# Two 256-column weight chunks multiplied as one 512-column operand, token tile by token tile, at the start of stages and in differential attention

## The reference

```python
def swiglu(x, wg, wu, wd):                       # 4 times, hidden width 2816
    return (jax.nn.silu(x @ wg) * (x @ wu)) @ wd

def sq_relu_mlp(h, w1, w2):                      # 4 times, hidden width 4096
    return jnp.square(jax.nn.relu(h @ w1)) @ w2

def diff_mixer(h, w_in, lam_p, norm_g, w_out, lambda_init, cos, sin):
    proj = h @ w_in                              # 1024 x 3072: q, k, v
    q = partial_rope(proj[..., :hq].reshape(b, t, DIFF_HEADS, 2, DIFF_D), cos, sin)
    k = partial_rope(proj[..., hq:2 * hq].reshape(b, t, DIFF_HEADS, 2, DIFF_D), cos, sin)
    v = proj[..., 2 * hq:].reshape(b, t, DIFF_HEADS, 2 * DIFF_D)
    lam = jnp.exp(jnp.sum(lp[0] * lp[1])) - jnp.exp(jnp.sum(lp[2] * lp[3])) + lambda_init
    o = diff_attention(q, k, v, lam)
    ...
    return o.reshape(b, t, hq) @ w_out

def second_block(x, ...):
    for i in range(4):                           # mixers: gdn, mlstm, diff, gdn
        x = x + rms_norm(mixer(rms_norm(x)), ...)
        x = x + rms_norm(sq_relu_mlp(rms_norm(x), mlp_w1[i], mlp_w2[i]), ...)
```

## Time and profile before

| what | value |
|---|---|
| median of 3 runs | 2362.12 us (2359.69 to 2362.32) |
| the profiled execution | 2360.35 us, its span 2358.6 us |
| PE busy | 2325.4 us, 99%, x16820 |
| DVE busy | 1567.7 us, 66% |
| ACT busy | 1157.1 us, 49% |
| POOL busy | 159.1 us, 7% |
| granted clock of PE | 0.999 |
| DMA | 405.14 MB, mean 172 GB/s |

### The profile page before, as it was taken

One profiled execution on the slowest core, in us unless ns is written; L12 is line 12 of the kernel. 1 busy time (PEld: TensorE's weight loads), 2 busy tenths in 40 slices (PEclk: granted clock), 3 DMA queues, 4 the chain that ended last, 5 costly groups with the idle time before them and its releaser, 6 DMA issues. The chain is left out here.

```text
span 2358.6 us, 39266 instructions
## 1 busy us (share of the span) xinstructions
PE 2325.4 (99%) x16820; PEld 2062.5 (87%) x16820; DVE 1567.7 (66%) x2133; ACT 1157.1 (49%) x1573; POOL 159.1 (7%) x177
## 2 busy tenths in 40 slices
PE   9999999999999999999999999999999999999998
PEld 8889888888889888899888899888898888998887
DVE  5566775666576865768666657766677656867665
ACT  5444744435435644466554445534465334665432
POOL 0100000020000100002210000100001001012000
PEclk9999999999999999999999999999999999999999
DMA  7766355666655466453265644556445565433662
GB/s 247 244 214 137 108 186 189 214 187 214 209 148 150 127 210 208 145 168 109 73 214 189 205 154 143 181 194 213 154 142 177 187 206 156 139 110 108 205 210 94
DMA packets 320829, 405.14 MB, mean 172 GB/s; under 512 B 48720, under 2 KB 281264, under 8 KB 320656
## 3 DMA queue, kind: packets, MB, share of 16 engines
q1 hardware_dynamic: 314992, 383.50, 51.6%
q0 software_dynamic: 5664, 19.13, 2.6%
HBM read 401.55 MB, written 1.05 MB: 171 GB/s over the span
## 5 line engine op out<-in xcount | busy, mean ns | idle before, releaser
L468 DVE TENSOR_TENSOR w_lo<-raw,w_hi 128x2048 fp32r<-128x2048 f32 (+1 forms) x355 | 796.4, 2267 | 60.5 <-ACT w_hi L461 59.6
L461 ACT CAST w_hi<-raw 128x2048 fp32r<-128x2048 f32 (+1 forms) x355 | 672.1, 1894 | 303.4 <-PE ps L484 227.6
L512 PE MATMUL ps<-aT,w_hi 128*128 128x512 f32 x2048 | 511.3, 392 | 0.0
L512 PEld LDWEIGHTS ps<-aT,w_hi 128*128 128x128 f32 x2048 | 373.3, 188 | 70.2
L482 PE MATMUL ps<-w_hi,h_hi 128*128 128x512 f32 x864 | 339.2, 393 | 0.7 <-DVE h_lo L1970 0.6
L483 PE MATMUL ps<-w_lo,h_hi 128*128 128x512 f32 x864 | 337.4, 391 | 0.0
L484 PE MATMUL ps<-w_hi,h_lo 128*128 128x512 f32 x864 | 336.3, 389 | 0.0
L482 PE MATMUL ps<-w_hi,aT 128*128 128x256 f32 (+2 forms) x992 | 300.6, 303 | 6.8 <-DVE aT L910 4.6
L514 PEld LDWEIGHTS ps<-aT,w_lo 128*128 128x128 f32 x2048 | 279.4, 190 | 20.0
L484 PE MATMUL ps<-w_hi,aT 128*128 128x256 f32 (+2 forms) x992 | 294.0, 296 | 0.0
L483 PE MATMUL ps<-w_lo,aT 128*128 128x256 f32 (+2 forms) x992 | 294.0, 296 | 0.0
(11 more groups left out here) (397 smaller groups left out, 2687.0 us busy)
## 6 DMA issues: line engine op xcount, KB each, us to landing
raw<-in_mlp_w SPq DMA_DIRECT2D x124, 1024.0 KB, 5.3
raw<-in_ffn_wg SPq DMA_DIRECT2D x43, 1024.0 KB, 5.3
raw<-in_ffn_wu SPq DMA_DIRECT2D x43, 1024.0 KB, 5.3
raw<-in_ffn_wd SPq DMA_DIRECT2D x40, 1024.0 KB, 4.9
raw<-in_gdn_w_in SPq DMA_DIRECT2D x32, 1024.0 KB, 5.9
raw<-in_mlstm_w_in SPq DMA_DIRECT2D x12, 1024.0 KB, 5.4
raw<-in_diff_w_in SPq DMA_DIRECT2D x12, 1024.0 KB, 5.2
raw<-in_w_in SPq DMA_DIRECT2D x8, 1024.0 KB, 5.2
```

Source lines behind the costliest of these rows:

```text
L461: nc.scalar.copy(used_part(hi_slot(n), n), used_part(raw_slot(n), n)).then_inc(hi_ready, 1)
L468: nc.vector.tensor_tensor(used_part(lo_slot(n), n), used_part(raw_slot(n), n), used_part(hi_slot(n), n).bitcast(F32), ALU.subtract).then_i ...
L512: nc.tensor.matmul(ps[:, bank + ft, :], hi[:, k, c], aT[:, k, :], start=k == 0, stop=False)
```

## The change

A new function `open_paired` takes the place of `open_stage` in both mixers of the first block, in the three feed-forward stages of the first block behind the first, in all four MLPs and in differential attention. Bank t now holds tile t of both chunks (one in each half), where bank c held both tiles of chunk c. Tile 0 begins as before, four k of each chunk apart; from then on `pair_steps` multiplies both chunks at once: high parts of two neighbouring slots are read as one operand of 2 x 256 columns. Where the two low parts stand in other order than the high ones (a ring of 5 slots beside one of 4), the low matmul stays two of 256. `weights_used` counts both chunks at the end of the pair. In stages that begin inside the norm of the first block, three pair steps stand ahead of the turns of tile 1, else two.

Differential attention also pairs its chunks 2, 3 and 8, 9, with ACT copying by tile. In the MLP the second hidden tile is now turned inside the first rows chunk (bank 7), and the fifth chunk's product waits for its low part in the middle; DVE and ACT take up its split behind those of chunk n0+6. The mixers 1 to 3 of the second block have their first turns inside the last bank of the MLP ahead (`turn_mixer`), one half of tile 0 (both in differential attention), and `open_stage` takes two steps more ahead of tile 1's turns in the mlstm mixer and the last gdn mixer.

```diff
+    def pair_steps(pe, n, t, steps):
+        swapped = slots_swapped(n)
+        both = ps[:, t, :].rearrange("p (a c) -> p a c", a=2)
+        for k in steps:
+            hi = of_both(w_hi, turn_of[n] % SPLIT, SPLIT, k)
+            x_hi, x_lo = (x_part[:, k, t * P:(t + 1) * P] for x_part in (aT_hi, aT_lo))
+            nc.tensor.matmul(both, x_hi, hi, start=k == 0, stop=False)
+            if swapped[0] == swapped[1]:
+                nc.tensor.matmul(both, x_hi, of_both(w_lo, lo_at[n], RAW, k), start=False, stop=False)
+            else:
+                for a in range(2):
+                    nc.tensor.matmul(ps[:, t, pair_half(n, a)], x_hi, by_cols(lo_slot(n + a))[:, k, :], start=False, stop=False)
+            last = nc.tensor.matmul(both, x_lo, hi, start=False, stop=k == KT - 1)
+        return last
...
+    def open_paired(pe, n, edge, first_tile=None):
...
+        turned_set(0)
+        pe.wait_ge(lo_ready, splits_made[n])
+        one_part(pe, n, 0, 0, first)
+        if edge["early"]:
+            turned_set(1)
+            one_part(pe, n, 0, 0, second)
+        pe.wait_ge(lo_ready, n + 2)
+        one_part(pe, n, 1, 0, first)
+        if edge["early"]:
+            turn_tile(pe, edge, 1)
+            one_part(pe, n, 1, 0, second)
+        else:
+            turned_set(1)
+            ahead = 7 if edge.get("late") else 6
+            pair_steps(pe, n, 0, range(4, ahead))
+            turn_tile(pe, edge, 1)
+            last = pair_steps(pe, n, 0, range(ahead, KT))
...
+        turned_set(2)
+        pair_steps(pe, n, 1, first)
+        turned_set(3)
+        pair_steps(pe, n, 1, second).then_inc(weights_used, 2)
...
     def mlp_tensor(pe, i, edge):
-        def turn_two():
-            turn_hidden(pe, hid0, 0, 2)
-            turn_hidden(pe, hid0 + 1, 1, 6)
-        open_stage(pe, n0, edge)
+        inside = {2: lambda: turn_hidden(pe, hid0, 0, 2), 3: lambda: pe.wait_ge(hid_lo, hid0 + 2)}
+        open_paired(pe, n0, edge)
...
-                hidden_rows(pe, n0 + u, hid0 + s, s)
+                hidden_rows(pe, n0 + u, hid0 + s, s, (lambda: turn_hidden(pe, hid0 + 1, 1, 7)) if s == 0 else None)
...
-            if s == 3:
-                pe.wait_ge(hid_lo, hid0 + 2)
...
     def mlp_vector(dve, i):
...
             for c in split_ahead(MLP_ORDER, u):
                 split_low(dve, n0 + c)
+            if (kind, s) == ("rows", 0):
+                turned_hidden_vector(dve, hid0 + 1, 1, 7)
+                hidden_split(dve, hid0 + 2, 2)
...
+    DF_PAIRED = (0, 2, 8)
...
+            if u in DF_PAIRED:
+                pe.wait_ge(lo_ready, splits_made[n0 + u + 1])
+                pair_steps(pe, n0 + u, 0, range(KT)).then_inc(df_tile.sem, 1)
+            elif u - 1 in DF_PAIRED:
+                pair_steps(pe, n0 + u - 1, 1, range(KT)).then_inc(weights_used, 2)
+            else:
+                tokens_product(pe, n0 + u, u % 2)
...
+    def mixer_turns(q):
+        return ((1, 0), (2, 0)) if factor_behind(q) else ((2, 1),)
```

More of the change, by code:

```diff
@@ new lines, in one_part @@
+    def one_part(pe, n, a, t, steps):
+        hi, lo = by_cols(hi_slot(n + a)), by_cols(lo_slot(n + a))
+        s = slice(t * P, (t + 1) * P)
+        for k in steps:
+            product(pe, ps[:, t, pair_half(n, a)], aT_hi[:, k, s], aT_lo[:, k, s], hi[:, k, :], lo[:, k, :],
+                    a == 0 and k == 0, a == 1 and k == KT - 1)
+    def open_paired(pe, n, edge, first_tile=None):
+        xpass = edge["xpass"]
+        turned_set = lambda e: pe.wait_ge(aT_lo_set.sem, aT_lo_set.count(xpass, e))
+        first, second = range(0, 4), range(4, KT)
+        if not edge["early"]:
+            turn_tile(pe, edge, 0, edge.get("begun", 0))
+        turned_set(0)
[15 more added lines that the diff above has]
+            last = pair_steps(pe, n, 0, range(ahead, KT))
+            if first_tile is not None:
+                last.then_inc(first_tile, 1)
+        turned_set(2)
+        pair_steps(pe, n, 1, first)
+        turned_set(3)
+        pair_steps(pe, n, 1, second).then_inc(weights_used, 2)
@@ L611, in open_stage @@
         tokens_part(pe, n, 0, 0, 1)
+        ahead = 2 if edge.get("late") else 0
+        tokens_steps(pe, n + 1, 1, 0, range(4, 4 + ahead))
         turn_tile(pe, edge, 1)
-        tokens_part(pe, n + 1, 1, 0, 1)
+        tokens_steps(pe, n + 1, 1, 0, range(4 + ahead, KT))
         open_second(pe, n, turned_set)
@@ L636, in last_rows @@
                 for r in range(2):
+                    if b == 3 and mixer_next is not None and (q, r) in mixer_turns(mixer_next):
+                        turn_mixer(pe, mixer_next, mixer_turns(mixer_next).index((q, r)))
                     if b == 3 and turn_next is not None and (q, r) in turns:
@@ L898, in turn_bank, with turned_scalar @@
         last.then_inc(turned.sem, 1)
-    def turned_scalar(act, xpass, t):
-        for half in range(2):
+    def turned_scalar(act, xpass, t, halves=(0, 1)):
+        for half in halves:
             act.wait_ge(turned.sem, turned.count(xpass, 2 * t + half))
@@ L1774, in addnorm_scalar @@
         early = a % 6 == 0
+        inside = range(len(mixer_turns(a + 1))) if into_mixer else ()
         for b in range(4):
@@ L1784, in addnorm_scalar @@
                 x_squares(act, a + 1, 0)
+                turned_scalar(act, xpass, 0, inside)
         if into_mixer:
-            turned_scalar(act, xpass, 0)
+            turned_scalar(act, xpass, 0, [half for half in range(2) if half not in inside])
             x_squares(act, a + 1, 1)
@@ L3339, in prenorm_edge @@
                         half_ready=lambda pe, t, half: pe.wait_ge(mlp_w.sem, mlp_w.count(q // 2, 2 * t + half)))
-        return dict(xpass=xpass, src=H, scaled=not factor_behind(q), early=False, fill={} if q else {(0, None): 3, (1, None): 8}, ready=lambda pe, t: pe.wait_ge(pre_done.sem, pre_done.count(q // 2, t)))
+        return dict(xpass=xpass, src=H, scaled=not factor_behind(q), early=False, begun=len(mixer_turns(q)) if q else 0,
+                    late=q and not factor_behind(q), fill={} if q else {(0, None): 3, (1, None): 8}, ready=lambda pe, t: pe.wait_ge(pre_done.sem, pre_done.count(q // 2, t)))
     def order_of_stages():
```

116 lines of the change are left out of this document (75 added, 41 removed).

## The result

The changed kernel takes 2374.94 us (median of 4 runs, 2373.13 to 2375.66), the one before 2361.11 in the same comparison: a ratio of 1.0058, 95% interval 1.004 to 1.0075. So it is slower by 13.8 us, where 2.4 faster was forecast, and outside the range. The profiled execution has a span of 2372.9 us, 14.3 longer than before.

What follows compares the result with a forecast made beforehand. PE was taken to bound the kernel, busy 2325.4 of 2358.6 us. Gains of 7.8 us less 4.4 in the MLPs and 1.0 in the third feed-forward stage made 2.4 saved: 2359.7 us, range 2353.5 to 2364.5.

Steps and rivals of the forecast that it cites:

- Merged matmuls: In all pair steps, 384 merges of two 256-column matmuls into one of 512, 0.013 us each: 5.1 us saved.
- Openings inside the first block's norm: Both mixers and three feed-forward stages: PE's waits for x go, 3.4 us saved, of which merges are 2.1.
- The wait for the low part: In the profiled norm opening, PE newly waits 0.5 us for the first low part, behind tile 1's turns.
- Turns inside, differential attention: Differential attention's first turns go into the MLP's last bank, chunks pair: 1.9 us saved, 2.2 with the MLP opening behind.
- the wait for ACT's copy at the third chunk: In differential attention, PE waits about 1 us there, where it waited 0.16 before.
- Third feed-forward stage: In the first block, n0+5 lands later: PE waits 0.7 us, and 0.3 at the next chunk, 1.0 in all.
- First turns inside at the mlstm mixer: PE's 0.51 us wait for the first low part is covered: 0.6 us saved; 0.9 with the MLP opening behind.
- The late release in an MLP: Slots freed 2.9 us later, n0+5 lands at T + 6.3 (T: opening's end): 4.4 us lost in four MLPs.
- The chain: In an MLP, from n0+5's landing through ACT's split and copy and DVE's splits to the hidden low part: 9.3 us.
- upper bound of 10.4: The most that later slot release was counted to cost in the four MLPs together, 10.4 us.
- the second rival: In the MLPs, n0+6's landing takes over n0+5's whole delay: 12.3 us lost against 7.8, 2366.6 us; chance 0.11.
- 7.8 of gains without losses: Norm openings 3.4, MLP openings 1.3, first turns at two mixers 1.2, differential attention 1.9: 7.8 us saved.

Runs made afterwards that it cites:

- second experiment: The changed kernel with POOL's two gain loads at each MLP issued only when the MLP's twelfth chunk is used: 2358.17 us, ratio 0.9984.
- first experiment: The changed kernel with the second hidden tile's ACT copy and DVE low part moved ahead of the weight splits in the MLPs: 2358.43 us, ratio 0.9986.
- fourth: The kernel before, with only the slots of an opening's first chunk released later, together with the second's: 2368.48 us, ratio 1.0029.
- tenth experiment: The kernel before with 40 small matmuls at its start and nothing else changed: 2359.93 us, ratio 0.9991.

## Why the prediction was wrong

The forecast is off by 16.2 us: 6.4 of waits in the MLPs, 6.7 behind them, 3.0 in the fourth block's gdn mixer, the rest small.

- **Merged matmuls: right in kind, a third too much.** 384 merges, wide ones 0.227 us apart. Undoing them cost about two thirds of 0.013 us each in the stretches where nothing else moved. (384 times 0.013 is 5.0 and not 5.1; nothing hangs on it.)
- **Openings inside the first block's norm: right.** The waits for x went, the opening of the earlier trace rows takes 12.5 us as worked out, and the five openings gain 3.1 us, 3.4 in the forecast. The wait for the low part in it is 0.3 and not 0.5.
- **Turns inside, differential attention: right as a sum.** -2.3 us against -2.2; the wait for ACT's copy at the third chunk came, with 0.5 and not 1. The price of the turns alone stayed open.
- **Third feed-forward stage: wrong in size.** 1.0 us was counted for waits. The one wait for w_lo is 0.2, and the stage behind its opening is 0.5 longer.
- **First turns inside at the mlstm mixer: right.** The stretch gains 0.7 where 0.9 was forecast, merges included.
- **The late release in an MLP: the step that failed.** The chain was right in place, members and length. Its start was not: "At 406 GB/s half a MB is 1.3 us: n0+5 lands at T + 6.3". The second experiment measures 3.0 us for it. The rate was read in a microsecond in which only weights move; the first gain load has the engines nearly to itself and moves half as much, and the second, in three of the MLPs, was not counted. So each MLP waits 2.2 to 3.5 us in place of 0.8 to 1.2, 10.8 in place of 4.4, just above the upper bound of 10.4. That this sum lies near that bound is luck: the second rival named this size of wait by another way in, n0+6's late landing. DVE's two splits run without a gap, so it was n0+5 that decided. The harm came of the order: with the low part ahead of the splits (first experiment), or with the same late landing and the old order (fourth), no such wait arises.
- **The clock: a step that was missing.** The forecast priced a wait at its length. With three of the four waits the granted clock fell to 0.50 for 3 us and more, 6.7 us in all behind the waits, and with the wait filled it did not. No term and no rival had it, though PE's granted clock of 0.999 was the first thing read.
- **The instruction count: another missing step.** Fewer matmuls moved the places of PE's instruction loads, and with them a wait in the fourth block's mixer: 3.0 us more than forecast. The trace of the kernel before had a sign of it, four waits for nothing shown, 2.7 us in all.

With the waits in the MLPs mended by the order, and with them the clock, and the mixer's wait gone by luck of the count, the changed kernel is 8.3 us faster than the one before (ratio 0.9964). That this is near the forecast's 7.8 of gains without losses is partly luck too: in the gdn mixers some of it is to be had without the change (tenth experiment).

## What to carry to other kernels

Where a release comes later, look for what stands behind the loaded data in the in-order queues of the engines that prepare it: moving one 0.7 us instruction of DVE (and ACT's copy for it) ahead of two splits was worth 16.5 us. A new wait of PE of the size seen here (about 2 us and more) is to be priced above its length, since the clock may fall with it. Before a change of a few us is judged in a kernel whose PE runs many short matmuls, shift its instruction count once and measure again: here 16 matmuls of 0.07 us made the kernel of the first experiment some 5 us faster, more than the merges were worth.

## What was not expected of the hardware

- With waits of PE of 2.36, 2.22 and 3.49 us the granted clock was 0.50 for 3.4, 3.4 and 6.8 us; with one of 2.71 it stayed at 1.00. 10 matmuls of 0.22 us in the wait kept it at 1.00.
- The first gain load of 0.5 MB, one row spread over 128 partitions from the software queue, keeps the DMA engines 0.99 busy at 223 GB/s; weight loads alone move 406, and the second such load, beside weights, 412 for its share of the engines.
- PE stood up to 3.7 us in a mixer with runs of 64 to 128 matmuls that start 0.015 us apart on average, each time until 1.2 to 1.6 us after a packet of its instruction queue; 16 more matmuls 2050 us earlier took that away.
